# Padded queries for the level products of a gated recurrence, and five places of small products moved, in a fused two-layer decoder step

## What is computed

```
S_t = f_t * S_(t-1) + k_t v_t^T        (64 x 64 state, decayed per key channel)
o_t = q_t S_t
so for the prompt   att[t,s] = sum_c q_t[c] k_s[c] * prod(f_(s+1)..f_t)[c],   o = att v
for the 8 samples   o = q (f * S_cache + k v^T)
```

## Time and profile before

| | us |
|---|---|
| median of 3 runs (829.32, 829.39, 827.66) | 829.32 |
| the profiled execution | 829.25 |
| its span (first to last instruction) | 827.5 |
| TensorE busy | 816.1 |
| VectorE busy | 570.0 |
| ScalarE busy | 436.8 |
| GpSimd busy | 264.2 |

### The profile page before, as it was taken

How to read it: one execution, slowest core, us unless ns; L and a number is a source line. 1 busy time by engine, 2 the same in 40 slices (tenths; PEclk the granted TensorE clock), 3 DMA queues, 4 the chain that set the end, 5 groups by cost and what they waited for, 6 DMA issues and landing times.

```text
span 827.5 us, 18120 instructions
## 1 busy us (share of the span) xinstructions
PE 816.1 (99%) x7016; PEld 801.4 (97%) x7016; DVE 570.0 (69%) x768; ACT 436.8 (53%) x621; POOL 264.2 (32%) x230
## 2 busy tenths in 40 slices
PE   9999999999999999999999999999999999999995
PEld 8999999999999999999999999999999999999995
DVE  7778787676877666554576688957787776645553
ACT  6553376645557665434353634774555666643442
POOL 4585282036710000121147825801565000001220
PEclk9999999999999999999999999999999999999999
DMA  9896859767657778776659968887665876776751
GB/s 314 235 319 256 301 162 324 237 227 269 218 179 253 240 241 306 248 262 226 205 164 247 312 234 278 241 259 256 232 237 179 260 247 221 260 280 234 250 203 52
DMA packets 171035, 200.00 MB, mean 242 GB/s; under 512 B 19680, under 2 KB 168496, under 8 KB 169648
## 3 DMA queue, kind: packets, MB, share of 16 engines
q1 hardware_dynamic: 169584, 197.02, 72.4%
q10 hardware_dynamic: 1392, 2.15, 0.7%
HBM read 191.25 MB, written 51.90 MB: 294 GB/s over the span
## 4 chain that ended last, share of the span: by engine, by line
PE 95%; DVE 3%; DMA 0%; ACT 0%; issue 0%; DVEq 0%; ACTq 0%
PE main L644 28%; PE main L645 28%; PE main L646 27%; PE small L694 2%; PE small L660 1%; PE small L646 1%; PE small L645 1%; PE small L644 1%; DVE w_lo L1189 1%; PE small L705 1%; DVE h_lo L1205 0%; DMA raw<-in_w_in 0%; PE small L798 0%; PE small L853 0%; PE small L722 0%; PE main L615 0%
## 5 line engine op out<-in xcount | busy, mean ns | idle before, releaser
L954 ACT ACTIVATE w_hi<-raw 128x1024 fp32r<-128x1024 f32 (+1 forms) x256 | 266.2, 1041 | 247.9 <-PE main L646 186.9
L1189 DVE TENSOR_TENSOR w_lo<-raw,w_hi 128x1024 fp32r<-128x1024 f32 (+1 forms) x256 | 337.3, 1318 | 64.6 <-ACT w_hi L954 60.6
L644 PE MATMUL main<-h_hi,w_hi 128*128 128x264 f32 x1264 | 365.6, 289 | 0.9 <-DVE w_lo L1189 0.8
L645 PE MATMUL main<-h_lo,w_hi 128*128 128x264 f32 x1264 | 358.8, 284 | 0.0
L646 PE MATMUL main<-h_hi,w_lo 128*128 128x264 f32 x1264 | 358.6, 284 | 0.0
L644 PEld LDWEIGHTS main<-h_hi,w_hi 128*128 128x128 f32 x1264 | 238.7, 189 | 5.9 <-DVE w_lo L1189 1.7
L645 PEld LDWEIGHTS main<-h_lo,w_hi 128*128 128x128 f32 x1264 | 239.0, 189 | 0.2
L646 PEld LDWEIGHTS main<-h_hi,w_lo 128*128 128x128 f32 x1264 | 237.6, 188 | 0.0
L644 PE MATMUL main<-a_hi,w_hi 128*128 128x264 f32 x512 | 145.3, 284 | 0.0
L645 PE MATMUL main<-a_lo,w_hi 128*128 128x264 f32 x512 | 145.0, 283 | 0.0
L646 PE MATMUL main<-a_hi,w_lo 128*128 128x264 f32 x512 | 145.0, 283 | 0.0
(11 more groups left out here) (222 smaller groups left out, 1030.0 us busy)
## 6 DMA issues: line engine op xcount, KB each, us to landing
raw<-in_w_in SPq DMA_DIRECT2D x48, 1024.0 KB, 5.8
raw<-in_w_up SPq DMA_DIRECT2D x32, 1024.0 KB, 5.3
raw<-in_w_down SPq DMA_DIRECT2D x32, 1024.0 KB, 5.2
out_kvs<-in_cache SPq DMA_DIRECT2D x48, 512.0 KB
out_kvs<-in_cache SPq DMA_DIRECT2D x32, 496.0 KB
raw<-in_w_o SPq DMA_DIRECT2D x8, 1024.0 KB, 5.3
raw<-in_w_br SPq DMA_DIRECT2D x8, 768.0 KB, 5.1
gates<-q_scratch SPq DMA_DIRECT2D x4, 768.0 KB, 7.2
```

Of the source, the lines that this page charges most:

```text
L644: pe.matmul(out[:, 0:TOK], wh, rh, start=start and k == 0, stop=False)
L645: pe.matmul(out[:, 0:TOK], wh, rl, start=False, stop=False)
L954: act.activation(w_hi[:, slot(l, u), 0:k, :], raw_of(u, k), ACT.Copy).then_inc(w_hi_ready, 1)
L1189: dve.tensor_tensor(w_lo[:, slot(l, u), 0:k, :], raw_of(u, k), w_hi[:, slot(l, u), 0:k, :].bitcast(F32), ALU.subtract).then_inc(w_lo_ready, 1)
```

## The change

1. Levels 1 to 8 and level 0: GpSimd (level 0: ScalarE) writes the queries of the two heads side by side, each with zeros on the other head's 64 partitions (`q_bd` in the space of `v_cache`, `q_lv`). One product with all 128 rows of keys then gives both heads. Level 1 takes the keys from `kg` directly. A level from 1 on now uses one bank and one mask.
2. Sample recurrence: the same with `q_st`; the state of one tile and sample is loaded once for two query columns.
3. Five moves: state 18 to 19; sample keys' transposes 20 to 21; scores part 2 from 23 to 22; two key transposes 26 to 28; attend 33 to 35. The copies that read them on ScalarE and VectorE move by as much, but for the masks of the scores, which stay.
4. Layer 0: units 6 and 7 are also made by `unit_lo_last`; VectorE makes w_lo of unit 6 before the bounds and that of unit 7 before the decays; the DMA of the first piece of weights is issued ahead of that of the gain.

```diff
@@ TURNS
-    + [f"level {i} {h}" for i in range(9) for h in range(2)]
+    + ["level 0 0", "level 0 1"]
+    + [f"level {i}" for i in range(1, 9)]
@@ tiles
+            q_st = sb("q_st", [P, 2, SAMPLES, 2], stack=early)
-                q_lv = sb("q_lv", [P, 2, 2, PROMPT], stack=s)
+                q_lv = sb("q_lv", [P, 2, 2, 2, P], stack=s)
-                att = sb("att", [P, 2, 4, P], stack=s)
+                att = sb("att", [P, 4, 2, P], stack=s)
+        q_bd = v_cache[:, :, :, :].rearrange("p b g c -> p (b g c)")[:, 0:4 * PROMPT].rearrange(
+            "p (h a t) -> p h a t", h=2, a=2)
@@ TensorE, level
-                            mm = pe.matmul(out, kk, qq, start=True, stop=True)
+                if i == 0:
...
+                    for hp in range(2):
+                        bank = use_bank(pe, l, f"level 0 {hp}")
+                        for tb in range(2):
+                            ts = slice(tb * P, tb * P + P)
+                            mm = pe.matmul(bank[:, tb * 2 * P:(tb + 1) * 2 * P], kg[:, hp, ts], q_bd[:, :, hp, ts],
+                                           start=True, stop=True)
...
+                    if i == 8:
+                        mm = pe.matmul(bank[:, hp * 2 * P:(hp + 1) * 2 * P], k_lv[:, 0, hp, 0:P], q_lv[:, 0, :, hp, :],
+                                       start=True, stop=True)
+                        continue
+                    early = P - LEVELS[i - 1]
+                    for tb in range(2):
+                        keys = kg[:, hp, :] if i == 1 else k_lv[:, i % 2, hp, :]
+                        c = (hp * 2 + tb) * P
+                        mm = pe.matmul(bank[0:early, c:c + P], keys[:, tb * P:tb * P + early],
+                                       q_lv[:, i % 2, :, hp, tb * HALF:(tb + 1) * HALF], start=True, stop=True)
@@ TensorE, between
-                if u == 18:
+                if u == 19:
                     pe.wait_ge(k_tm_ready, l + 1)
                     bank = use_bank(pe, l, "state")
-                if u == 20:
+                if u == 21:
                     z_ready(pe, l, CT_V + 2)
-                for j, gs in enumerate((range(NG), (0, 1), (2,))):
-                    if u == 21 + j:
+                for at, j, gs in ((21, 0, range(NG)), (22, 1, (0, 1)), (22, 2, (2,))):
+                    if u == at:
                         scores(l, j, gs)
-                            for h in range(2):
-                                rows = slice(h * HD, (h + 1) * HD)
-                                mm = pe.matmul(bank[rows, hp * SAMPLES + b:hp * SAMPLES + b + 1],
-                                               state_s[rows, b, hp, :], z[rows, CT_CQ + hp, PROMPT + b:PROMPT + b + 1],
-                                               start=True, stop=True)
+                            c = (hp * SAMPLES + b) * 2
+                            mm = pe.matmul(bank[0:HD, c:c + 2], state_s[:, b, hp, :], q_st[:, hp, b, :],
+                                           start=True, stop=True)
-                for at, g in ((24, 0), (26, 1), (26, 2)):
+                for at, g in ((24, 0), (28, 1), (28, 2)):
-                if u == 33:
+                if u == 35:
                     pe.wait_ge(kv_tm_ready, l * NG + NG)
                     attend(l)
-                if u == 35:
                     pe.wait_ge(s_probs, l + 1)
-                    if l == 0 and u < 6:
+                    if l == 0 and u < 8:
                         pe.wait_ge(out_taken, u + 1)
                         unit_lo_last(u, main[u % 4]).then_inc(w_used, 1)
+                        between(l, n)
                         continue
@@ ScalarE
+                if u == 5:
+                    z_ready(act, l, CT_CQ + 1)
+                    act.wait_ge(q_zeroed, l + 1)
+                    for h in range(2):
+                        rows = slice(h * HD, (h + 1) * HD)
+                        act.activation(q_bd[rows, h, :, :], z[rows, CT_CQ:CT_CQ + 2, 0:PROMPT], ACT.Copy)\
+                           .then_inc(q_bd_ready, 1)
+            act.dma_start(piece_raw(0), piece_source(0)).then_inc(piece_landed[0], 16)
             act.dma_start(cur[:, C_G1:C_G1 + KT], io["gain0"]).then_inc(gain_in, 16)
-            for i in range(3):
+            for i in range(1, 3):
@@ VectorE, step 3
+                        split_lo(l, at + 3)
                         if l == 0:
                             bounds()
                             new_params()
-                        split_lo(l, at + 3)
+                            split_lo(l, at + 4)
@@ GpSimd
-                    pool.tensor_tensor(halves(q_lv[:, i % 2, :, :], 1), halves(z[:, CT_CQ:CT_CQ + 2, 0:PROMPT], 1),
-                                       halves(cum_f[:, :, :], 1), ALU.mult)
+                    scaled = pool.tensor_tensor(
+                        q_lv[:, i % 2, :, :, :].rearrange("p h a (n t) -> p h (a n) t", t=half),
+                        q_bd.rearrange("p h a (n s t) -> p h (a n) s t", s=2, t=half)[:, :, :, 1, :],
+                        late.unsqueeze(1).to_broadcast([P, 2, PROMPT // half, half]), ALU.mult)
+                    if i > 1:
+                        scaled = pool.tensor_tensor(halves(k_lv[:, i % 2, :, :], 0), halves(kg[:, :, 0:PROMPT], 0),
+                                                    halves(suf_f[:, :, :], 0), ALU.mult)
```

More of the change, by code:

```diff
@@ L677, in queries @@
-                def queries(qq, tb):
-                    if not i:
-                        return qq[:, tb * P:tb * P + P]
-                    return qq[:, tb * P:tb * P + P].rearrange("p (n s t) -> p n s t", s=2, t=LEVELS[i - 1])[:, :, 1, :]
-                w = HALF if i else P
-                early = P - LEVELS[i - 1] if 0 < i < 8 else P
-                banks = [use_bank(pe, l, f"level {i} {h}") for h in range(2)]
-                for hp in range(2):
-                    for tb in range(2 if i < 8 else 1):
-                        for h in range(2):
-                            kk, qq = operands(hp, h)
-                            if i == 8:
-                                out, kk, qq = banks[h][:, hp * P:hp * P + P], kk[:, 0:P], qq[:, P:2 * P]
-                            else:
-                                c = (hp * 2 + tb) * w
-                                out, kk, qq = banks[h][0:early, c:c + w], kk[:, tb * P:tb * P + early], queries(qq, tb)
-                            mm = pe.matmul(out, kk, qq, start=True, stop=True)
-                            if hp == 1 and (i == 8 or tb == 1):
-                                done(mm, f"level {i} {h}")
+                    pe.wait_ge(q_bd_ready, l * 2 + 2)
@@ new lines, in level @@
+                    for hp in range(2):
[4 more added lines that the diff above has]
+                                           start=True, stop=True)
+                        done(mm, f"level 0 {hp}")
+                    return
+                pe.wait_ge(level_ready, l * 8 + i)
@@ L698, in scores @@
+                done(mm, f"level {i}")
             def scores(l, j, gs):
@@ L996, in between @@
                        .then_inc(sigmoids, 1)
+                if u == 5:
[5 more added lines that the diff above has]
+                           .then_inc(q_bd_ready, 1)
+                if u == 6:
+                    act.wait_ge(q_st_zeroed, l + 1)
+                    for h in range(2):
+                        rows = slice(h * HD, (h + 1) * HD)
+                        act.activation(q_st[rows, :, :, h], z[rows, CT_CQ:CT_CQ + 2, PROMPT:TOK], ACT.Copy)\
+                           .then_inc(q_st_ready, 1)
                 if u == 8:
@@ L1014, in between @@
                 if u == 16:
[L1015 to L1018 removed]
+                    copy_bank(l, "level 8", att_far[:, :, :, :].rearrange("p a h c -> p (a h c)"),
+                              lambda b: b[:, :], far_ready)
+                    freed("level 8", far_ready, l + 1)
                 if u == 18:
@@ L1271, in mask_level @@
                         dve.wait_ge(att_clear, l + 1)
-                    for h in range(2):
-                        name = f"level {i} {h}"
+                    for hp in range(1 if i else 2):
+                        name = f"level {i}" if i else f"level 0 {hp}"
                         bank = take(dve, l, name)
```

73 lines of the change are left out of this document (34 added, 39 removed).

## The result

The changed kernel takes 833.6 us (median of four runs, 833.25 to 834.87) against 828.5 for the kernel before (four runs beside it). The ratio is 1.0064, with a 95% interval of 1.0046 to 1.0082. The forecast was 827.4 with a range to 829.8, so it has the wrong sign and the range misses the time. The profiled execution of the changed kernel spans 831.5 us, the one before 827.5: 4.0 us to explain where -1.8 was expected.

What follows compares the result with a forecast made beforehand. TensorE, busy 99% of the span, was taken as the bound. Terms -1.8 + 0 - 0.2 - 0.4 + 1.1 - 1.0 + 0.2 + 0.3 summed to -1.8 us, from 829.25 to 827.4; range 825.0 to 829.8.

Steps and rivals of the forecast that it cites:

- Levels 0 to 8 on TensorE, -1.8: Full-array level products lose their edges: levels 1 to 6 save, levels 0, 7 and 8 cost more; -1.8 us, two layers.
- rule on packing: 64-row products in distinct row groups run concurrently; by it unpacking gives +0.04 us for each of levels 1 to 7, total near 831.
- GpSimd, +0.3: Doubled query products use up GpSimd's lead over TensorE at the levels; stall 0 to 1 us a layer, +0.3 in all.
- Rival C: GpSimd's query products, also stretched by VectorE's splits, lengthen its level rounds; total over 831 us; chance 0.1 together with D.
- D: Full-array products cannot hide their loads, so levels 1 to 6 save nothing; total 831 us; chance 0.1 together with Rival C.
- The state's place, -0.2: State moved beside its neighbour exits into transposes instead of a main product: -0.1 us each, -0.2 in all.
- Scores, +1.1: Scores 2 directly behind scores 1 waits for banks that VectorE frees late; +0.55 to 0.6 us, +1.1 for both layers.
- Attend, -0.4: Attend and sample probabilities share a place, so one exit and one entry become one switch; -0.2 us, -0.4 in all.
- sample recurrence, 0: 32 two-column products' worth of records replace 64 one-column records, no time change taken; bounds 0.93 us saved and +0.5.
- Start, -1.0: In layer 0 TensorE no longer stands for w_lo before units 6 and 7; -1.0 us.
- Gain, +0.2: The gain's DMA, behind the first weight piece, may delay the first scaling up to 0.8 us, 0.5 reaching TensorE; +0.2 taken.
- The clock (rival A): 1.2 GHz falls behind the sample recurrence, 1.7 us each: none 825.7, two 829.1; chances 0.2 and 0.2, each shared with another rival.

Runs made afterwards that it cites:

- light_queries: The changed kernel with GpSimd multiplying only the first head's queries in every level (256 elements instead of 512): 826.3 us, 0.9967 of the kernel before.
- start_only: The kernel before with only the new order of the first low halves on TensorE and VectorE, gain requested as before: 826.9 us, ratio 0.9983.

## Why the prediction was wrong, point by point

- **Levels 0 to 8 on TensorE, -1.8:** right where TensorE didn't wait, to 0.02 us for each level, level 0's +0.44 and level 7's 1.22 included (light_queries). The Trainium skill's rule on packing (page "TensorE: Matmul & The Clock Gate", section "Part 3: Packing small matmuls"), which the prediction sets against it, would have given +0.04 for a level; the trace does not bear it out for these products: 0.88 against 1.23.
- **GpSimd, +0.3: the step that failed first.** It measured 2.9 us at the levels, 1.95 in layer 0 and 0.98 in layer 1. The prediction's sum for one layer was 4.1 ahead, less 3.4 and 1.0, plus 0.9, less 1.0 for one stretched product: -0.4. It then took 0.3 for both layers, less than its own sum gives. In layer 1 the parts come out near it: from the start of level 3 to the end of level 8's key product GpSimd took 22.8 us before and 26.4 after, 3.6 more where the parts give 3.5. But the release by level 1 gave GpSimd back 0.1 and not 0.4, so TensorE came 1.3 sooner to it, and the sum is -0.8. In layer 0 a term is missing that the text itself had named under the start ("Late next: the decays, by one split, and so GpSimd's first level") and then priced nowhere. GpSimd starts 1.2 us later and TensorE's first place comes 1.2 sooner (start_only has both): 2.4 us of head start, of which some 0.8 were paid. The copies on ScalarE, for which GpSimd waits in layer 1, cost nothing there. Rival C was the right mechanism, with rounds of 4.7 us against the 4.55 by the sum, and I gave it, with D, one chance in ten.
- **The state's place, -0.2: the step that wasn't there.** It measured +2.6. I asked who waits for GpSimd's level products, and never who shares its time. The row with the answer stood in my own group: a product of 0.74 us took 1.74 beside a split. I read it as a stretch of one product; it was the other engine's turn, and it works both ways.
- **Scores, +1.1:** +1.3, by the mechanism forecast (a wait of 0.78 us behind VectorE's second mask, in both layers; 1.6 in the list of waits above). **Attend, -0.4, and sample recurrence, 0:** as forecast.
- **Start, -1.0:** -1.3, and start_only confirms it in the time. **Gain, +0.2:** +0.85. I had allowed for a scaling up to 0.8 later, 0.5 of it reaching TensorE. It came 1.37 later: the gain's transfer took 4.2 us from issue to landing behind a piece of 256 KB on its queue, and 2.3 before.
- **The clock (rival A):** the fall behind the sample recurrence of layer 0 is gone, and one has come in layer 1. The sums over three stretches, after (the earlier trace rows before; the last three numbers are the granted clock, the DMA share and GB/s):

```profile
104.00:106.60 2.60, 2.60 (x37) 2.58 (x37) 2.54 (x3) 1.17 (x2) 2.60 (x2) 1.00 0.84 236
106.60:109.00 2.40, 2.40 (x22) 2.40 (x21) 2.17 (x3) 0.19 (x1) 2.40 (x2) 1.00 0.03 10
510.80:513.80 3.00, 3.00 (x18) 3.00 (x17) 2.85 (x3) 0.60 (x1) 3.00 (x2) 0.59 0.25 73
```

The sample recurrence of layer 0 lies 2.5 us later than before, so the second row is the stretch behind it: the granted clock is 1.00 (2.4 GHz) there, as in the first, where it was 0.50. It is 0.59 on average from 510.8 to 513.8, with both levels in it. So the profiled execution has one such fall in each kernel, and the clock is not what made the change slower. Which version has fewer falls over many runs stays open.

In the sum, by terms of the prediction: GpSimd +2.6 against the forecast, the state's place +2.8, the gain +0.65, scores +0.2, the start -0.3, in all some 6 us from -1.8 to the measured 4.0.

## What to carry to other kernels

When a change makes work on GpSimd longer or later, list every VectorE instruction that will lie beside it and add the whole of one to the other, then follow VectorE's chain to the next thing that TensorE needs. A head start of one engine on another is a stock, and the buffers between them cap it: what lies above the cap is spent in a wait (2.73 us in layer 1), and below it the length of a round decides, on each side. Before removing time from a 98% busy engine, find the chain with the least slack at the next meeting point. Here it was VectorE's, lengthened by GpSimd's products: with those short (light_queries) all that was saved at the levels stayed saved, with them long it was paid back behind.

## What the runs showed of the hardware

- VectorE and GpSimd exclude each other for whole products with both inputs in SBUF: six in a row end one after the other, with 1.22 us becoming 2.24, 1.80 becoming 3.20, 1.30 becoming 2.89. A VectorE evacuation with one input in PSUM, in the midst of it, was not held up (0.42 us).
- A transfer of 4 KB took 4.2 us from issue to landing behind one of 256 KB issued 0.53 us before it on the same queue, and 2.3 us ahead of it.
- Full-array FP32 products have no edge between main products (0.88 us for 8 records of 128 columns), but with 64 output columns they cost 0.34 us more (1.22, level 7).
- 32 records of two columns over the full height take as long as 64 of one column on half the height (2.03 us, as in the earlier trace rows; L798 in layer 1, after):

```profile
508.47 2.03 PE L798 MATMUL small<-q_st,state_s 128*64 128x2 f32 x32
```
